# A three-part fp32 product: GpSimd's remainder splits issued in quarters and placed elsewhere in its queue, one split moved to VectorE

## The reference

```
def gmlp_mixer(h, ...):                       # layer 0
    proj = h @ w_in                           # 1024 -> 6144
    u, v, z = gelu(...), gelu(...), proj[..., 4096:]
    v = layer_norm(v, ln_g, ln_b)
    y = u * (w_masked @ v + b_s) * silu(z)
    return y @ w_out                          # 2048 -> 1024
def dilated_attention_mixer(h, ...):          # layer 1
    proj = h @ w_in                           # 1024 -> 10240
    for g in range(3): o_g, lse_g = dilated_window_attention(rope(q), rope(k), v)
    alpha = softmax over g of lse_g
    o = sum_g alpha_g * o_g
    return (o * silu(z)) @ w_out              # 1024 -> 1024
x = x + rms_norm(mixer(rms_norm(x)))          # for each layer
```

## Time and profile before

| | |
|---|---|
| median of 3 runs | 1620.79 us (1620.33 to 1624.49) |
| profiled execution | 1625.27 us, its span 1623.5 us |
| granted TensorE clock, mean | 0.98 |
| busy: PE, DVE, ACT, POOL | 1513.9 (93%), 759.1 (47%), 574.9 (35%), 375.3 us (23%) |
| chain that ended last | PE 62%, DMA 20%, DVE 11%, ACT 3% |

### The profile page before, as it was taken

One profiled execution on the slowest core, in us unless ns is written; L12 is line 12 of the kernel. 1 busy time (PEld: TensorE's weight loads), 2 busy tenths in 40 slices (PEclk: granted clock), 3 DMA queues, 4 the chain that ended last, 5 costly groups with the idle time before them and its releaser, 6 DMA issues.

```text
span 1623.5 us, 23323 instructions
## 1 busy us (share of the span) xinstructions
PE 1513.9 (93%) x9552; PEld 1050.3 (65%) x9552; DVE 759.1 (47%) x1293; ACT 574.9 (35%) x779; POOL 375.3 (23%) x101
## 2 busy tenths in 40 slices
PE   5999999999999799999999998898989999999996
PEld 2788888887667444444334433587877778788785
DVE  2678887566436712121111111616216545345993
ACT  2431335544432312122112111353333455455551
POOL 0000000011000110000000000286766565555551
PEclk9999999999999999999999999999989999999998
DMA  8632225344767899999999999375435433433330
GB/s 311 209 129 80 78 85 178 130 133 155 285 238 285 342 404 420 422 421 422 422 422 422 422 422 421 139 264 182 155 130 181 155 131 130 142 118 131 129 117 26
DMA packets 120876, 381.10 MB, mean 235 GB/s; under 512 B 9302, under 2 KB 11134, under 8 KB 96222
## 3 DMA queue, kind: packets, MB, share of 16 engines
q1 hardware_dynamic: 120798, 380.02, 62.3%
HBM read 378.95 MB, written 1.05 MB: 234 GB/s over the span
## 4 chain that ended last, share of the span: by engine, by line
PE 62%; DMA 20%; DVE 11%; ACT 3%; issue 2%; SPq 1%; POOL 1%; DVEq 0%; POOLq 0%; ACTq 0%
DMA arena<-in_w_exp_up 17%; PE ps L786 10%; PE ps L787 10%; PE ps L793 10%; PE ps L1207 7%; PE ps L968 3%; PE ps L967 3%; PE ps L974 3%; PE ps L1219 2%; PE ps L867 2%; DVE arena L2309 1%; DVE arena L2311 1%; ACT w_hi L2505 1%; PE ps L887 1%; DVE arena L1464 1%
## 5 line engine op out<-in xcount | busy, mean ns | idle before, releaser
L2429 POOL TENSOR_TENSOR w_lo<-ring,w_hi 128x2048 fp32r<-128x2048 f32 x71 | 335.0, 4745 | 187.5 <-ACT w_hi L2505 187.5
L2505 ACT ACTIVATE w_hi<-ring 128x2048 fp32r<-128x2048 f32 x130 | 247.1, 1912 | 325.0 <-PE ps L793 142.3
L786 PE MATMUL ps<-w_hi,xt_hi 128*128 128x512 f32 x512 | 204.2, 399 | 7.0 <-ACT w_hi L2505 4.7
L787 PE MATMUL ps<-w_hi,xt_lo 128*128 128x512 f32 x480 | 189.1, 394 | 0.0
L1538 DVE TENSOR_TENSOR w_lo<-ring,w_hi 128x2048 fp32r<-128x2048 f32 x59 | 134.8, 2286 | 89.5 <-ACT w_hi L2505 89.2
L786 PE MATMUL ps<-w_hi,yt_hi 128*128 128x512 f32 x352 | 141.6, 402 | 6.7 <-DVE yt_lo L1531 2.7
L2092 DVE TENSOR_SCALAR selT<-ps 128x256 fp32r<-128x256 f32 x32 | 13.6, 424 | 247.2 <-ACT arena L2836 247.2
L1207 PE MATMUL ps<-arena 128*32 128x512 f32 x1056 | 118.7, 593 | 11.0 <-DMA arena<-in_w_exp_up 11.0
L793 PE MATMUL ps<-w_lo,xt_hi 128*128 128x512 f32 x512 | 126.9, 390 | 1.0 <-POOL w_lo L2429 1.0
L1207 PE MATMUL ps<-ring,arena 128*32 128x512 f32 x992 | 111.7, 593 | 11.2 <-DMA ring<-in_w_exp_up 10.1
L786 PEld LDWEIGHTS ps<-w_hi,xt_hi 128*128 128x128 f32 x512 | 97.4, 190 | 32.5 <-ACT w_hi L2505 5.1
(11 more groups left out here) (323 smaller groups left out, 2456.4 us busy)
## 6 DMA issues: line engine op xcount, KB each, us to landing
ring<-in_w_in SPq DMA_DIRECT2D x40, 1024.0 KB, 5.2
ring<-in_b_w_in SPq DMA_DIRECT2D x40, 1024.0 KB, 5.1
arena<-in_w_exp_gate SPq DMA_DIRECT2D x33, 1024.0 KB, 23.0
arena<-in_w_exp_up SPq DMA_DIRECT2D x33, 1024.0 KB, 25.0
arena<-in_w_exp_down SPq DMA_DIRECT2D x32, 1024.0 KB, 23.3
ring<-in_w_exp_down SPq DMA_DIRECT2D x32, 1024.0 KB, 23.3
ring<-in_w_exp_gate SPq DMA_DIRECT2D x31, 1024.0 KB, 23.0
ring<-in_w_exp_up SPq DMA_DIRECT2D x31, 1024.0 KB, 25.0
```

What stands on the lines that cost most here:

```text
L786: pe.matmul(o[:, tt, :], hi[:, k, x_], w[:, c, :], start=(bias is None and j == 0 and c == 0), stop=False)
L787: pe.matmul(o[:, tt, :], lo[:, k, x_], w[:, c, :], start=False, stop=False)
L2429: pool.tensor_tensor(w_lo2[:, slots_of[n]], ring[:, slots_of[n]], w[:, :, :].bitcast(F32), ALU.subtract).then_inc(S("w_lo_full"), 1)
L2505: act.activation(part_of(n)[1][:, :, :], ring[:, slots_of[n]], ACT.Copy).then_inc(S("w_hi_full"), 1)
```

## The change

GpSimd makes each of its remainders as four instructions of 128x512 instead of one of 128x2048; the semaphore is raised by the last. VectorE takes the remainder of the first output unit, behind the fourth `join_ahead`. GpSimd makes the remainder of the first attention unit behind the first token tile's power, that of the second unit behind the second tile's power, and those of the other three output units only when both halves of the gated output are ready (`b_o_ready` at 2). The keep-busy matmuls go from 50 to 24 at both layer entries (`turn_tokens` serves both), and from 70 to 12 at the output.

```
-        by_vector = split + [first["a"] + 2, first["a"] + 3, first["b"] + 2]
+        by_vector = split + [first["a"] + 2, first["a"] + 3, first["b"] + 2, first["b_out"]]
 ...
-                    stay_busy(o, 50)
+                    stay_busy(o, 24)
 ...
-                    stay_busy(claim(("oT", c)), 70)
+                    stay_busy(claim(("oT", c)), 12)
 ...
                         join_ahead(c)
+                        if c == 3:
+                            own_remainder(first["b_out"])
 ...
-                    pool.tensor_tensor(w_lo2[:, slots_of[n]], ring[:, slots_of[n]], w[:, :, :].bitcast(F32), ALU.subtract).then_inc(S("w_lo_full"), 1)
+                    for k in range(UC):
+                        ins = pool.tensor_tensor(w_lo2[:, slots_of[n], k, :], ring[:, slots_of[n], k, :], w[:, k, :].bitcast(F32), ALU.subtract)
+                    ins.then_inc(S("w_lo_full"), 1)
 ...
             powers(both)
+            remainders_to(first["b"])
+            powers(one_by_one[:1])
+            remainders_to(first["b"] + 1)
+            powers(one_by_one[1:])
             remainders_to(first["b"] + 2)
-            powers(one_by_one)
             pool.wait_ge(S("x_normed"), 4)
             powers(both)
+            remainders_to(first["b_out"])
+            pool.wait_ge(S("b_o_ready"), 2)
             remainders_to(len(units))
             powers(one_by_one)
```

## The result

| | before | after |
|---|---|---|
| median of 5 runs each | 1622.28 us (1620.33 to 1624.49) | 1609.84 us (1607.39 to 1612.75) |
| profiled execution | 1625.27 us, span 1623.5 | 1607.49 us, span 1605.7 |
| busy: PE, DVE, POOL | 1513.9, 759.1, 375.3 us | 1496.4, 713.0, 419.0 us |

The ratio is 0.9919, with a 95% interval of [0.9904, 0.9934]: 12.4 us faster by the medians, 2.4 us beyond the forecast of 1612.2, in the predicted range. The two spans differ by 17.8 us, but 2.9 us of that arise before the experts' last matmul (1026.39 us before, 1023.48 after), where the two programs do the same.

The account below looks back on a forecast made before the run. TensorE's pace was taken to bound most of the second half, VectorE, waiting on whole GpSimd remainders, the attention's end. Terms sum to -8.6 us: 1616.7 from the profiled 1625.27, less 4.5 to the median, 1612.2; range 1600 to 1621.

Parts of the forecast that it names:

- gMLP's entry: Start of the gMLP: fewer keep-busy matmuls free at most 0.75 us, the later power (0.8 us) eats it: 0.
- gMLP's input: gMLP's input units: cuts make TensorE 7.9 us later, the vanished 4.66 us gap and 1.64 give back: 1.6 lost.
- gMLP's output: gMLP's output: a longer pair of remainders runs into the last gating step, 0.5 us lost.
- attention's entry: Start of the attention: VectorE's remainder of tile 0 comes 1.8 us later, one more slow TensorE group costs 0.5.
- wait on `w_lo` behind it: After the attention's entry: TensorE's wait for GpSimd's first remainder grows from 0.31 to 2.0 us, 1.7 lost.
- score step: Attention's score step at 1323 us: the 2.68 us gap shrinks, 0.7 us gained.
- attention's end: From 1500 us: VectorE's waits shorten; gains of 0.8, 4.1 and 9.1 us in TensorE's gaps, 14.0 in all.
- I take 5.35: GpSimd's remainder in four quarters: 5.35 us, each cut costing some 0.28, between bounds of 4.52 and 6.2.
- The cuts are free: Rival: a remainder stays at 4.6 us and GpSimd keeps its lead; -21 us, 1600 us; chance 0.25.
- GpSimd becomes the bound: Rival: 0.55 us a cut, 6.2 us a remainder, so slower by about 6: 1626.6 us; chance 0.10.
- Quarters don't let VectorE in: Rival: GpSimd holds on over back-to-back instructions, each VectorE step waits 5.35 us; 1620 us; chance 0.07.
- The mishap named under "wrong": Sign against the forecast: the maxima's and the join's small steps wait for quarters, leaving the end on VectorE.

Follow-up runs that it names:

- three other executions of the same code: The changed kernel repeated (1608.9 us), without GpSimd's hold for the gated output (1609.16 us), and with GpSimd making the output's first remainder (1606.75 us); same instructions until about 1550 us.
- the two with the hold: The changed kernel repeated (1608.9 us) and the changed kernel with GpSimd making the output's first remainder (1606.75 us); both keep GpSimd's wait for the gated output.
- 50 at the entries: Changed kernel with 50 keep-busy matmuls again at both layer entries and 12 kept at the output; 1607.18 us, ratio to before 0.991.
- both powers first: On the changed kernel with 50 entry keep-busy matmuls: first attention unit's remainder ahead of both powers, the second unit's behind both; 1601.27 us, ratio 0.9877.
- mixed kernel: On the kernel with both powers first and 50 at the entries: whole remainders where no long VectorE step stands beside them, quarters elsewhere; 1599.15 us, 0.9865.
- the remainder on GpSimd: Changed kernel with the first output unit's remainder made by GpSimd behind its hold, not by VectorE; 1606.75 us, ratio 0.9906.

## Why the prediction was right, and where it was off

| term of the sum | predicted | measured | in the three other executions of the same code |
|---|---|---|---|
| gMLP's entry | 0 | +1.1 | +1.1 to +2.2 |
| gMLP's input | +1.6 | -2.6 | -2.0 to -3.0 |
| gMLP's output | +0.5 | +1.1 | -0.6 to +1.3 |
| attention's entry | +2.3 | +0.6 | -0.1 to +0.8 |
| wait on `w_lo` behind it | +1.7 | +1.4 | +1.4 |
| score step | -0.7 | -2.1 | -2.1 |
| attention's end | -14.0 | -14.3 | -14.3, -14.4 (the two with the hold) |
| sum | -8.6 | -14.9 | -12.8, -15.9 (the two with the hold) |

The sum is that of the unrounded terms. All are counted against the one profiled execution of before, which took longer than its kernel's median (1625.27 us against 1622.28).

**The mechanism held.** VectorE's two-input steps wait for one GpSimd instruction, so their price follows its length: wholes, halves and quarters give a ladder for L2311 (4.9, 2.72, 1.66 us), and quarters alone, everything else untouched, give 0.994. The Trainium skill (SBUF — State Buffer, "Who interferes with whom") has a VectorE instruction with two SBUF inputs and a GpSimd instruction that reads SBUF exclude each other for a whole instruction. This ladder agrees. The cover and what is late next were right too. The gap before L1370 went from 2.18 to 1.49 us, with ScalarE's evacuation (L2890) ahead of it in the chain (0.7 gained, 0.8 predicted); the gap before `join_last`'s unit went with its slow start; and the path through keep-busy matmuls, transposes, copy and remainder took 4.55 us (4.9 predicted). That end was put at 14.0 us "at almost any length of a quarter", and halves give 14.1 there too (+3.5 behind the score step, -10.6 at the first output matmul).

**The mis-sized term is the gMLP's input**, through "I take 5.35". A remainder takes 5.00 us back to back (35.02 / 7), so a cut costs 0.14 us, not 0.28: the pair of 128x1024 that I read it from the earlier trace rows is another kernel line with other operands. The 0.47 us that a VectorE step costs GpSimd was right (0.44). Those 0.35 us a remainder matter beyond their sum, because they decide whether GpSimd gains on TensorE's 5.44 us. At 5.35 it gains 0.1 a unit, and I wrote that it "just keeps up"; at 5.00 it gains 0.44, or 3.1 us over the seven. The working then reads: the four units beside the norm cost 6.77 us each (5.00 + 4 x 0.44), 1.33 above TensorE's pace, so 5.3; plus 0.4 for the first; less 3.1: 2.6 us of waiting in place of 7.9. The trace has 1.13 + 0.17 + 1.02 + 1.07 = 3.4, less the 0.70 of before, so 2.7. With the 4.66 + 1.64 us that the vanished gap gives back, the term is -3.6; measured are -2.6. Of the 1.0 us between them, 0.4 is the `w_lo` groups behind three more waits than before (2.11 us instead of 1.98), and the rest I did not settle. That the gap would vanish was right: the load left at 1111.22. The forecast did not say how short the instructions must be for that: with halves 3.89 us of the gap are left.

**The entries.** At the gMLP's entry I looked only for what the shorter keep-busy run would free, found nothing, and wrote 0. It costs 1.1 us: TensorE reaches L828 0.4 us earlier, but after a wait of 1.85 us, and the two groups from there run slowly (1.98 and 1.90 us, not 1.20 and 1.09). The runs with 50 at the entries show it for this layer (-0.4 to +0.2 us); at the attention's entry 50 and 24 don't differ. The attention's entry lost less than predicted: `rest_tokens` came only 0.5 us late, not 1.8. The first power came 0.9 us sooner than I had put it (218.1 us behind the experts' last matmul, not 219.0), and the way from the second power to `rest_tokens` took 4.5 us instead of 5.0. That the remainder between the two powers delays them is what the run with both powers first shows (it gains 4.4 us on the kernel before from the gMLP's end to the first full unit, where 50 at the entries alone lose 0.2). I priced it at 1.8 us among the losses; at 4.6 us it is the largest fault of the change.

**The score step** gained 2.1 and not 0.7: the gap shrank by 0.9, and the matmuls behind it, slow before (2.79 us for twelve), take 1.50. That second part is not shown to come of the change: with whole remainders, placed as changed, the gap is still 2.63 us, and the twelve take 1.50 all the same. Of all thirteen profiled executions only that of the kernel before has them slow, so 1.3 us of the term may be chance in the trace that everything is counted from.

**The rivals.** "The cuts are free" was half true: 5.00 lies midway between 4.58 and 5.35, and the time between that rival's 1600 and the forecast, much nearer to the forecast. "GpSimd becomes the bound" needed 0.4 us a cut and is out. "Quarters don't let VectorE in" is out for two-input steps. The mishap named under "wrong" did occur once, at no cost in time: in the fourth `join_ahead` three small merging steps wait for a quarter each. VectorE's timeline of the changed kernel:

```profile
1554.15 1.04 DVE L2288 TENSOR_TENSOR arena<-arena 128x8 f32<-128x8 f32 x1
1555.22 1.21 DVE L2289 TENSOR_TENSOR arena<-arena 128x8 f32<-128x8 f32 x1
1556.47 1.37 DVE L2291 TENSOR_TENSOR arena<-arena 128x8 f32<-128x8 f32 x3
```

A step of 128x8 takes 0.16 us alone. TensorE was busy until 1566.60, so this stayed off the path.

## What to carry to other kernels

Where a GpSimd stream runs beside chains of two-input VectorE steps, cut its instructions near those chains and leave them whole elsewhere: in this kernel a cut costs 0.14 us, and each such step then waits for a part instead of the whole. Before pricing a slower engine, compare its pace with that of the engine it feeds: 5.00 or 5.35 against 5.44 us is a growing lead or none. After shortening what a run of keep-busy matmuls covers, shorten the run where the trace shows it ending last (here the output, 6.3 us), but look first at what comes next. At the gMLP's entry the 50 ended last too, and 24 only moved TensorE's idle time to the next wait and cost 1 to 2 us. And put the small steps of a norm ahead of long work that is not urgent.

## What the runs showed of the hardware that I had not expected

- A single-input step of two elements a partition (L2199, 128x2) took 4.77 us beside quarters and 2.21 beside whole remainders. It started at 1091.5 and ended with the last of GpSimd's 28 back-to-back quarters (1096.2); with whole remainders it also ended with the last. There it was not let in between quarters as the two-input steps are. In the mixed kernel it was: it took 0.56 us and ended with the quarter under way, and two more followed back to back. L2233, of the same shape, took only 1.25 us beside quarters at 1234.5, so what tells them apart stays open.
- The first output unit, from its first `w_hi` to its first `w_lo` matmul, took 5.4 us in six kernels (the changed one, whole remainders, quarters alone, halves, 50 at the entries, the remainder on GpSimd) and 3.8 us in three (keep-busy as before, both powers first, mixed cuts); the repeat of the changed kernel took 5.4 again. All of these had the same 2.37 us gap ahead of it. TensorE's granted clock over 1560 to 1590 us is 0.94 in the changed kernel and 1.00 with the old keep-busy counts, so part of the unit ran at the lower of its two levels in the one and none in the other. Kernels with 12 keep-busy matmuls there stand on both sides, and so do kernels with 70. The gap alone does not decide it; what does was not found.
